# Around the routed experts: token rows turned and place numbers loaded ahead of the branch, two bodies instead of three, engines that leave the body one by one

## The reference, cut to what matters

```python
hl = modulate(xl, mod_l[3], mod_l[4])                 # 256 tokens x 1024
grp = argmax(hl @ w_rg + b_rg)                        # 1 group of 4
top_v, top_i = top_k(le[grp], 2)                      # 2 experts of its 8
w = p_grp * softmax(top_v)
yb = (silu(x[rows_e] @ w_eg[e]) * (x[rows_e] @ w_eu[e])) @ w_ed[e]   # for e in 0..31
yl = segment_sum(yb * w, token)                       # back to the token rows
xl = post_norm(xl, mod_l[5] * yl, ln2_g, ln2_b)
# next block
xl = modulate_2(xl, ...); xc = modulate_2(ctx, ...)   # then ffn1
```

## Time and profile before

| | us |
|---|---|
| median of 3 runs | 3386.48 |
| profiled execution, its own time | 3386.41 |
| its span, first to last instruction | 3384.5 |
| PE busy | 3059.8 (90%) |
| DVE busy | 1421.1 (42%) |
| ACT busy | 1079.3 (32%) |
| chain that ended last: PE | 82% |

### The profile page before, as it was taken

How to read it: one execution, slowest core, us unless ns; L and a number is a source line. 1 busy time by engine, 2 the same in 40 slices (tenths; PEclk the granted TensorE clock), 3 DMA queues, 4 the chain that set the end, 5 groups by cost and what they waited for, 6 DMA issues and landing times.

```text
span 3384.5 us, 43660 instructions
## 1 busy us (share of the span) xinstructions
PE 3059.8 (90%) x18812; PEld 2365.3 (70%) x18812; DVE 1421.1 (42%) x2098; ACT 1079.3 (32%) x1579; POOL 308.6 (9%) x309
## 2 busy tenths in 40 slices
PE   6988898779999969999888788999989999897998
PEld 4866798745555548787677546878768787773898
DVE  4655454522222233232476454333343333436554
ACT  4443353222222233222432233322242221434433
POOL 0024360200000000000104001000010000300000
PEclk9988899879999989999998899999999999999999
DMA  7557755469999933232339221323222323310353
GB/s 223 168 187 234 232 159 151 159 267 391 391 395 390 395 123 97 78 101 74 93 125 308 59 75 50 99 88 107 68 87 87 100 86 90 136 63 0 129 183 100
DMA packets 415220, 537.34 MB, mean 159 GB/s; under 512 B 14340, under 2 KB 389924, under 8 KB 390308
## 3 DMA queue, kind: packets, MB, share of 16 engines
q1 hardware_dynamic: 415012, 534.38, 46.3%
HBM read 533.30 MB, written 1.05 MB: 158 GB/s over the span
## 4 chain that ended last, share of the span: by engine, by line
PE 82%; DVE 8%; ACT 4%; DMA 3%; issue 2%; SPq 0%; POOL 0%; DVEq 0%; ACTq 0%; POOLq 0%
PE ps L188 79%; PE ps L187 2%; DVE ar L243 2%; ACT ar L313 2%; DVE LR L243 1%; DVE ar L259 1%; DMA RAW<-in_ada_w 1%; ACT HR L313 1%; DMA RAW<-in_w_in 1%; PE ps L194 1%; DVE ar L262 0%; DVE ar L253 0%; DVE ar L249 0%; ACT arf1i L313 0%; ACT AH L313 0%
## 5 line engine op out<-in xcount | busy, mean ns | idle before, releaser
L188 PE MATMUL ps<-AH,HR 128*128 128x512 f32 (+1 forms) x2552 | 900.7, 353 | 66.0 <-DVE AL L243 39.9
L188 PE MATMUL ps<-AL,HR 128*128 128x512 f32 (+1 forms) x2552 | 887.2, 348 | 0.0
L188 PE MATMUL ps<-AH,LR 128*128 128x512 f32 (+1 forms) x2552 | 886.0, 347 | 0.0
L243 DVE TENSOR_TENSOR LR<-RAW,HR 128x2048 fp32r<-128x2048 f32 (+3 forms) x232 | 487.3, 2102 | 599.8 <-ACT HR L313 597.9
L313 ACT ACTIVATE HR<-RAW 128x2048 fp32r<-128x2048 f32 (+3 forms) x232 | 404.1, 1744 | 771.8 <-PE ps L188 664.4
L188 PEld LDWEIGHTS ps<-AH,HR 128*128 128x128 f32 x2552 | 490.3, 192 | 138.3 <-ACT arf1i L313 19.8
L188 PEld LDWEIGHTS ps<-AL,HR 128*128 128x128 f32 x2552 | 490.6, 192 | 60.1 <-issue 1.9
L188 PEld LDWEIGHTS ps<-AH,LR 128*128 128x128 f32 x2552 | 490.1, 192 | 58.6
L188 PE MATMUL ps<-ar 64*128 64x128 f32 (+9 forms) x1318 | 236.8, 373 | 61.9 <-ACT ar L313 26.8
L249 POOL TENSOR_SCALAR X<-X 128x512 f32<-128x512 f32 (+2 forms) x50 | 83.8, 1701 | 2264.2 <-ACT AH L313 1630.6
L188 PEld LDWEIGHTS ps<-ar 64*128 64x128 f32 (+2 forms) x1318 | 140.9, 192 | 140.5 <-issue 44.7
(11 more groups left out here) (180 smaller groups left out, 3759.8 us busy)
## 6 DMA issues: line engine op xcount, KB each, us to landing
RAW<-in_ada_w SPq DMA_DIRECT2D x72, 1024.0 KB, 6.5
RAW<-in_f1i SPq DMA_DIRECT2D x44, 1024.0 KB, 5.1
RAW<-in_f2i SPq DMA_DIRECT2D x44, 1024.0 KB, 5.1
RAW<-in_w_in SPq DMA_DIRECT2D x32, 1024.0 KB, 5.7
RAW<-in_w_ada SPq DMA_DIRECT2D x24, 1024.0 KB, 8.1
RAW<-in_w_eu SPq DMA_DIRECT2D x17, 1024.0 KB, 9.9
HF<-in_w_ed SPq DMA_DIRECT2D x17, 1024.0 KB, 8.6
LF<-in_w_eu SPq DMA_DIRECT2D x17, 1024.0 KB, 9.6
```

The costliest lines, as they stand in the source:

```text
L188: return self.e.matmul(o, w, x, start=start, stop=stop)
L243: return self.e.tensor_tensor(o, a, b, op) if self.e else NOTHING
```

## The change

In the router part: PE turns the token rows right behind the logits, ACT copies their high halves ahead of its first exponential, DVE makes the low halves of the first two banks behind the mask. `iot` is loaded behind the router's constants, ahead of the expert weights. There are two flags and two bodies, `few` (at most 64) and `all`. In `few` DVE does the other two low halves and moves `selected(1)` back. At a body's end nobody meets: PE does one small matmul that raises `joined`, the others go on to the code behind the branch, where ACT, DVE and SyncE wait for `joined`. SyncE loads the first three tiles of the ring "rest" at the body's end, as soon as their slots are free.

```diff
 def route_sp(D, K):
     D.cst("triu", o.bsel).then_inc(K.loaded["sel"], 16)
+    D.cst("iotar", K.few.iot, n=130).then_inc(K.loaded["iotah"], 16)
 def route_pe(T, K):
     for j in range(2):
-        b, held = T.bank("logits", j)
+        b = bank(4 + j, "logits", j)
...
+    for q in range(2):
+        for j in range(2):
+            b = bank(2 * j + q, "htk", j, q)
+            T.turn(b, [(o.h32[:, 4 * q + m, j * 128:j * 128 + 128], 128 * m) for m in range(4)]
+                   ).then_inc(*pe("htk", j, q))
     T.wait_ge(*dve.of("mask"))
 def route_act(S, K):
     norm_act(S, K, "out1", o.XL, 256, 0, o.sq, o.rs, post)
+    for q in range(2):
+        for j in range(2):
+            S.wait_ge(*K.pe.of("htk", j, q))
+            S.act(K.few.rows(K.few.HTK.hi, j, q), K.few.turned(j, q), ACT.Copy).then_inc(*act("htk", j, q))
     S.wait_ge(*dve.of("group"))
 def route_dve(V, K):
     V.tt(o.bsel, o.bsel, K.ident[:, :], SUB).then_inc(*dve("mask"))
+    for j in range(2):
+        V.wait_ge(*act.of("htk", j, 0))
+        K.few.low_rows(V, j, 0).then_inc(*dve("htk", j, 0))
+        K.free(dve, "htk", j, 0)
     V.wait_ge(*pe.of("pos"))
...
-    then(V.ts(o.cnt[:, 1:2], o.cnt[:, 0:1], 64.0, None, ALU.is_le))
-    then(V.ts(o.cnt[:, 3:4], o.cnt[:, 0:1], 128.0, None, ALU.is_gt))
+    V.ts(o.cnt[:, 1:2], o.cnt[:, 0:1], 64.0, None, ALU.is_le).then_inc(*dve())
     then(V.ts(o.cnt[:, 2:3], o.cnt[:, 0:1], 64.0, None, ALU.is_gt))
-    then(V.tt(o.cnt[:, 2:3], o.cnt[:, 2:3], o.cnt[:, 3:4], SUB))
-    then(V.cp(o.flag[:, :], o.cnt[:, 1:4]))
+    then(V.cp(o.flag[:, :], o.cnt[:, 1:3]))
 def branch(P, K, *bodies):
-    flags = [... for i in range(3)]
-    for i, (name, body) in enumerate(zip(("few", "some", "all"), bodies)):
+    flags = [... for i in range(2)]
+    for i, (name, body) in enumerate(zip(("few", "all"), bodies)):
+def join(T, K):
+    T.mm(K.banks[0][:, 0:32], K.ident[:, :], K.ones[:, 0:32], True, True).then_inc(K.joined, 1)
+def rest_early(D, K):
+    D.enter("rest")
+    D.load(NSLOT)
+# class Few
+    def rows(self, x, j, q):
+        return x[:, j, :].rearrange("t (k m c) -> t m c k", k=8, m=8)[:, 4 * q:4 * q + 4]
+    def turned(self, j, q):
+        return self.banks[2 * j + q][:, :].rearrange("t (m c k) -> t m c k", m=4, c=16)
+    def low_rows(self, V, j, q):
+        return V.tt(self.rows(self.HTK.lo, j, q), self.turned(j, q), self.rows(self.HTK.hi.bitcast(F32), j, q), SUB)
 def few_sp(D, K):
-    D.cst("iotar", K.few.iot, n=130).then_inc(K.loaded["iotah"], 16)
     D.j = D.ring.depth
-    D.load(len(D.ring.plan))
-    meet(D, K, "end")
+    n = len(D.ring.plan)
+    D.load(n)
+    for j in range(n):
+        if j % D.ring.depth < NSLOT and j + D.ring.depth >= n:
+            D.wait_ge(*K.pe.of("w", "few", j))
+    rest_early(D, K)
 # few_pe, few_act: the 4 turns and the 4 copies leave; few_pe ends in join(T, K);
 # few_act, few_dve, few_pool end without a meet
 def few_dve(V, K):
     selected(0)
-    selected(1)
+    for j in range(2):
+        o.low_rows(V, j, 1).then_inc(*dve("htk"))
...
-    for j in range(2): for q in range(2): (wait for ACT, tt to HTK.lo, free)
     V.cp(o.pT[0:32, :], K.ps("pT")[0:32, 0:256]).then_inc(*dve("pT"))
+    selected(1)
 def after_act(S, K):   # and after_dve, and sync_program behind the branch
+    S.wait_ge(K.joined, 1)
```

More of the change, by code:

```diff
@@ L674, in __init__ @@
         self.parts = {p: {q: Tick(self.sem(f"{p}{q}_done")) for q in ("pe", "dve", "act", "pool")}
-                      for p in ("", "all_", "some_", "few_")}
+                      for p in ("", "all_", "few_")}
         self.part("")
-        for s in ("first", "x", "tri", "pool", "router", "sel", "ctx2", "iota", "iotah", "glam", "wg2", "rope", "rpb"):
+        for s in ("first", "x", "tri", "pool", "router", "sel", "ctx2", "iotah", "glam", "wg2", "rope", "rpb"):
             self.loaded[s] = self.sem(f"{s}_loaded")
@@ L682, in __init__ @@
         self.rings = {p: Ring(p, [self.sem(f"{p}_weights{i}") for i in range(NSLOT)], raws)
-                      for p in ("main", "all", "some", "rest")}
+                      for p in ("main", "all", "rest")}
         halves = ExitStack()
@@ L710, in __init__ @@
                      for i in range(2)]
-        self.stored = self.sem("stored")
+        self.stored, self.joined = self.sem("stored"), self.sem("joined")
         self.one, self.route = One(self), Route(self)
-        self.every, self.some, self.few = Every(self), Some(self), Few(self)
+        self.every, self.few = Every(self), Few(self)
         raws = raws + [t[:, i, :] for t in self.whole for i in range(t.shape[1])] + self.few.raws
@@ L1419, in __init__ @@
         self.pos, self.cnt = A.get(2, 32), A.get(4)
-        self.flag = K.sb("flag", [128, 3], mybir.dt.int32, self.ctx)
+        self.flag = K.sb("flag", [128, 2], mybir.dt.int32, self.ctx)
         self.XL = K.X[:, :, 256:512]
@@ L1448, in route_pe, with bank @@
     T.wait_ge(K.loaded["router"], 128)
-    for j in range(2):
-        b, held = T.bank("logits", j)
+    def bank(i, *name):
+        b, held = T.hold(i, *name)
         for w in held:
             T.wait_ge(*w)
+        return b
+    for j in range(2):
+        b = bank(4 + j, "logits", j)
         for k in range(8):
@@ L1456, in route_pe @@
         T.mm(b[:, 0:36], K.ones[0:1, 0:128], o.br[0:1, :], False, True).then_inc(*pe("logits", j))
+    for q in range(2):
[3 more added lines that the diff above has]
+                   ).then_inc(*pe("htk", j, q))
     T.wait_ge(*dve.of("mask"))
-    b, held = T.bank("pos")
-    for w in held:
-        T.wait_ge(*w)
+    b = bank(4, "pos")
     T.mm(b[:, 0:32], o.bsel, o.MK[:, 0, :], True, True)
@@ L1564, in branch @@
     meet(P, K, "route end")
-    flags = [P.e.value_load(K.route.flag[0:1, i:i + 1]) for i in range(3)] if P.e else None
+    flags = [P.e.value_load(K.route.flag[0:1, i:i + 1]) for i in range(2)] if P.e else None
     seen = P.seen
-    for i, (name, body) in enumerate(zip(("few", "some", "all"), bodies)):
+    for i, (name, body) in enumerate(zip(("few", "all"), bodies)):
         P.seen = {}
@@ L1595, in early_landed @@
 def early_landed(P, K):
+    P.wait_ge(K.loaded["iotah"], 16)
     for j in range(K.rings["few"].depth):
@@ L1668, in every_pe @@
     meet(T, K, "end")
+    join(T, K)
     T.lo, T.hi, T.holder = 0, 8, [None] * 8
@@ L1704, in every_act @@
     act.note("end")
-    meet(S, K, "end")
 def every_dve(V, K):
@@ L1737, in every_dve @@
     dve.note("end")
-    meet(V, K, "end")
 def every_pool(G, K):
@@ L1747, in every_pool @@
     K.pool.note("end")
[L1748 to L1772, removed]
@@ L1775, in some_sp @@
-def some_sp(D, K):
-    early_landed(D, K)
-    D.cst("iotar", K.some.iot, n=129).then_inc(K.loaded["iota"], 16)
-    D.load(len(D.ring.plan))
-    meet(D, K, "end")
[L1782 to L1800, removed]
@@ L1803, in some_pe @@
[L1803 to L1869, removed]
-                b = bank("ye", e, half)
-                for k in range(4):
-                    T.mm(b[:, :], h.hi[:, k, :], w.hi[:, k, :], k == 0, False)
-                    T.mm(b[:, :], h.hi[:, k, :], w.lo[:, k, :], False, False)
-                    m = T.mm(b[:, :], h.lo[:, k, :], w.hi[:, k, :], False, k == 3)
-                m.then_inc(*pe("ye", e, half))
-                pe.note("w", T.ring.name, j)
-        elif what == "scatter":
-            T.wait_ge(*act.of("ye", e, 1))
-            T.wait_ge(*dve.of("ye", e, 1))
-            T.wait_ge(*dve.of("selt", e))
-            for m in range(8):
-                y = K.banks[4 + m // 2][:, 256 * (m % 2):256 * (m % 2) + 256]
-                for x in (o.YE[e % 2].hi, o.YE[e % 2].lo):
-                    last = x is o.YE[e % 2].lo
-                    z = T.mm(y, x[:, m * 128:m * 128 + 128], o.SELT[e % 3][:, :], e == 0 and not last and m % 2 == 0,
-                             e == 31 and last, True)
-            z.then_inc(*pe("scatter", e))
-    pe.note("end")
-    meet(T, K, "end")
-    T.lo, T.hi, T.holder = 0, 8, [None] * 8
@@ L1893, in some_act @@
-def some_act(S, K):
-    o, pe, dve, act = K.some, K.pe, K.dve, K.act
-    early_landed(S, K)
-    for j in range(2):
-        for q in range(2):
-            S.wait_ge(*pe.of("htk", j, q))
-            S.act(o.HTK.hi[:, j, 512 * q:512 * q + 512], K.ps("htk", j, q)[:, :], ACT.Copy).then_inc(*act("htk", j, q))
-    for what, e in some_order():
-        i = e % 2
-        if what == "gather":
-            if e:
-                S.wait_ge(*pe.of("gu", 4 * e - 1, 1))
-            for k in range(8):
-                S.wait_ge(*pe.of("xg", e, k, False))
-                S.act(o.XG.hi[:, k, :], K.ps("xg", e, k, False)[:, :], ACT.Copy).then_inc(*act("xg", e))
-                K.free(act, "xg", e, k, False)
-        elif what == "gate_up":
-            for p in range(2):
-                S.take()
-                S.take()
-                S.wait_ge(*pe.of("gu", e, p))
-                if e:
-                    S.wait_ge(*dve.of("hid", e - 1, p))
```

(60 more changed lines are left out.)

71 lines of the change are left out of this document (removed).

## The result

The changed kernel took 3358.72 us (median of 4 runs, 3353.11 to 3362.47) against 3385.68 (4 runs, 3382.51 to 3387.32): ratio 0.9919, 95% interval 0.9907 to 0.993. The forecast was 3364.9 with a range of 3359 to 3373, so the median lies 0.3 us outside it and the gain, 27.0 us, is 5.5 us more than forecast. The profiled execution is the fastest of the four: 3353.11, span 3351.3.

What follows compares the result with a forecast made beforehand. PE, 90% busy, was taken to bound the kernel, so gains lie only where it stands still: 14.7 us at the entry plus 6.8 at the exit, 21.5 off 3386.4, giving 3364.9 us, range 3359 to 3373.

Steps and rivals of the forecast that it cites:

- Entry: Start of `few`: no DMA wait for place numbers left, PE gathers at 685.3 in place of 699.96; gain 14.7 us.
- Loop follows: Expert loop: PE sets the pace at 16.04 us an expert, so the loop ends 14.7 us earlier too.
- Rival C: Expert loop becomes bound by transfers; at 371 GB/s 32 experts cost 29 us, time 3394; chance 0.04.
- rival D: Entry: the place numbers still land late, held up with the weights; it would keep 10 us, 3375; chance 0.03.
- Behind the gathers: Gathers and loop run as before, at clock 0.50 until the gates have run some 3 us; no loss forecast.
- Rival B: Earlier, denser PE work brings the full clock sooner: gathers lose 4 us, first gates 1.5; 3359.4; chance 0.06.
- Exit: Behind the experts: without the meeting and with one body to pass, DVE goes on at 1230.0 against 1236.81; gain 6.8 us.
- My bound of 8.8: Exit's upper bound: passing the body takes less than the wait for `joined`, 1236.81 less 1228.0.
- Rival A: Exit's stall is for distance, not per body; only 2.3 us gained there, time 3369.4; chance 0.13.
- Early tiles: Exit: the tiles of "rest", issued 18 us before the engines leave, were in time before too; worth nothing.
- The sum: Whole kernel: 14.7 + 6.8 = 21.5 us gained, 3386.4 to 3364.9 us; chance 0.74.
- The forecast's 0.9 us: Router part: ACT's table load falls behind the four copies, so DVE goes on at 674.65, not 673.77; cost 0.9 us.

Runs made afterwards that it cites:

- e4: The kernel before with only the place numbers loaded ahead of the expert weights: 3376.81 us, ratio 0.9966.
- e2: The changed kernel (two bodies) with all engines meeting again at the end of `few`: 3363.28 us, ratio 0.9932.
- e1: The changed kernel with the third body and its flag back, not taken, engines still leaving one by one: 3367.45 us, ratio 0.9936.
- e7: The changed kernel with the first three tiles of "rest" loaded only behind the branch, once `joined` is up: 3366.9 us, ratio 0.9932.
- e5: The changed kernel again, file unchanged, for its scatter and a second trace: 3363.32 us (5 runs), ratio 0.993.
- e3: The changed kernel with both the third body and the meeting back, so the entry's change alone against the kernel before: 3373.4 us, ratio 0.9956.
- e6: The kernel before again, file unchanged, for a second trace: 3386.54 us, ratio 1.0.

## Why the prediction was right or wrong

- **Entry, 14.7 us forecast, 14.9 and 14.7 in the two pairs of traces.** The steps hold: the DMA wait goes, the low halves are hidden, the table load falls onto the path behind the copies. DVE went on 0.7 us later from the mark (20.65 against 19.97); forecast 0.9. The first copy begins 1.1 us behind the logits' end, as computed.
- **Loop follows.** It does: 505.7 us in every trace but e4's. Rival C did not come; rival D is refuted by e4, where the small load is not held up.
- **Behind the gathers, nothing forecast, 0.6 to 1.0 us lost.** The step "the loop runs as before, at clock 0.50 until the gates have run for some 3 us" was off. Before, the full clock came 3 us after the first gate (711.05, the windows read 0.50 up to 714); in the changed trace the gates start at 692.83 and the windows are:

```profile
692.00:698.00 6.00, 5.27 (x14) 1.66 (x15) 0.00 (x0) 0.60 (x1) 0.00 (x0) 0.50 0.14 23
698.00:700.00 2.00, 2.00 (x12) 0.81 (x10) 0.00 (x0) 0.90 (x1) 0.00 (x0) 0.98 0.82 315
```

  (stretch, its us, busy of PE, PEld, DVE, ACT, POOL, granted clock, DMA share, GB/s.) The clock was 1.2 GHz for 5 us of gates. Rival B had this the wrong way round. Behind the turns the full clock did come for some 3 us (0.93 from 667 to 671), but PE was busy for only 0.9 us of them.
- **Exit, 6.8 us forecast, 9.1 measured: the step that failed.** I kept 4.82 us as the price of the one body left, from a row in which all five engines pass at once and the body is the second. In e2, where it is the only one, the piece is 3.7 us with all five together; apart it costs ACT 2.5 us (2.8 in the second trace), and DVE 2.8 for the first body of e1. With that, DVE and ACT are behind the branch before `joined`, and the floor decides. My bound of 8.8 was that case; the matmul for `joined` took 0.15 us where I had put 0.3. The sequencers also run ahead of their last operation: ACT's compare is at 1206.6, when that operation has only started (1206.58), which I had left half open. DVE's compare is at 1207.3, 0.7 us ahead of the end of its last operation; of the 2.3 us by which the exit was short, 0.6 are this and 1.6 the price. Rival A is refuted by e2, where the piece is one and the exit 5.3 us shorter with the meeting in place.
- **Early tiles, nothing forecast:** shown by e7.
- **The sum.** 22.9 us against 21.5. The other 4 us of the 27.0 are scatter outside the change, which I had allowed 2.5 us for: e5's difference is 23.3. So the range was missed, by 0.3 us, by the draw of four runs (3353 to 3362; the second five lie at 3361 to 3367, and their median, 3363.32, is inside the range), while one term, the exit, was really 2.3 us short. Without that error the forecast of 3362.6 would have been 3.9 us off in place of 6.2.
- The Trainium skill ("Runtime: NRT & Kernel Launch", section "Instruction fetch mechanics") lays a far branch's stall to a fetch of the target's page by DMA. The trace agrees so far that such transfers are there. The DMA view has them as "instruction": none before the branch (1222 to 1227.6), and then, by queue (packets, MB, share of 16 engines), in the kernel before from 1222 to 1240:

```profile
q14 instruction: 10, 0.08, 3.1%
q8 instruction: 4, 0.07, 2.3%
```

  and in the changed kernel from 1204 to 1213:

```profile
q14 instruction: 4, 0.03, 1.4%
q8 instruction: 2, 0.03, 1.3%
```

  The shares come to 0.9 us a packet on q14 before and to 0.5 after, as if they hindered each other or met the weight loads that start at 1232.8. But in e2, with all five engines at once (q14: 6 packets, a share of 1.7% over 10 us), they take 0.45 us each, and ACT still stalls 3.7 us. So the transfers alone don't explain the price of branching together; the cause stays open.
- The drain that the Trainium skill ("ScalarE: Activation LUTs", section "What ACT_TABLE_LOAD costs") puts beside a load, 1.38 us, is not seen: the two exponentials start at 670.69, 0.01 behind the load. The forecast's 0.9 us was right to leave it out.

Open: why engines that branch together stall longer, why the second body passed costs more than the first (2.5 and 3.4 us on ACT apart, 4.3 and 5.0 together before), and why the stretches outside scatter. The scatter goes with the clock: of the nine runs of the changed kernel the two with a mean granted clock of 0.959 took 3353.1 and 3355.8 us, the seven at 0.954 to 0.956 took 3361.3 to 3367.2. In its two traces the clock from 300 to 400 us was 0.85 and 0.81. What makes the clock differ from run to run is not shown.

## What to carry to other kernels

Look for the small load that is issued behind the large ones and waited for at once: one line moved ahead took 10.6 us off the way to the first gather, and made the kernel 11.4 us faster by the medians (6.1 in its trace, where the clock took some back). At a branch, a price read where all engines stall together is not the price of one that goes at its own time, and the price of a second body is not that of a first; let each engine leave when it is done and join them by one semaphore. And where a kernel's runs scatter by 10 us, measure a change of 20 in its own stretch, from a mark in the same trace.

## What the runs showed of the hardware

- Passing a body that is not taken cost ACT 2.5 to 2.8 us where the engines left apart (five traces), and 3.4 for a second body (e1). Where five engines passed together it was 3.7 for one body (e2), and for two bodies 3.4 to 4.3 and then 5.0 to 5.3 (before, e3, e4, e6). On PE it was 3.3 to 3.6 us for the first body in all cases, and 4.7 to 4.9 for a second, so PE did not gain from leaving apart.
- Behind the compares of the exit the trace has DMA packets of the kind "instruction": in the changed kernel 4 between 1206.6 and 1210.5 (0.04 MB), none in the 2.6 us before.
- After a gap of 1.2 us in place of 9.8, PE's 16 mean matmuls behind the branch ran at the full clock in 3.72 us, before in 6.65. It was not on the path.
- One program gave 3381.4 to 3392.1 us in 17 runs on one chip, all with the same order of work; the mean granted clock was 0.954 in the shortest and 0.950 in the longest.
